# Freeing weight slots later, one more high buffer, and one unsplit fp32 chunk in each small expert of an MoE block

## The reference

```python
h = rms_norm(x, ffn_norm_g)                      # 512 x 1024
logits = h @ w_router + b_router                 # 32 experts, top 4 of each token, softmax over the 4
for e in range(32):                              # rows of h that chose expert e
    gu = xb @ w_gate_up[e] + b_gate_up[e]        # 1024 -> 2048
    gate, up = split(gu); gate = min(gate, 7); up = clip(up, -7, 7)
    act = (up + 1) * gate * sigmoid(1.702 * gate)
    y = (act @ w_down[e] + b_down[e]) * weight   # 1024 -> 1024, added to the token's row
```

## Time and profile before

| | |
|---|---|
| median of 3 runs | 1774.97 us (1774.8 to 1775.13) |
| profiled execution | 1766.66 us, span 1764.9 us |
| PE, DVE, ACT, POOL busy | 1698.8, 1381.7, 1200.8, 713.1 us |
| granted TensorE clock | 1.00 of full speed in the expert stage |
| moved by DMA | 504.64 MB, of them 384 chunks of 1 MB of expert weights |

### The profile page before, as it was taken

The page is one execution under the profiler, slowest core; times in us unless marked ns, Lnnn a source line. Parts: engine busy times, 40 slices in busy tenths (PEclk is TensorE's granted clock), DMA queues, the critical chain, the costliest instruction groups (busy, mean ns, idle before and its releaser), DMA issues.

```text
span 1764.9 us, 24895 instructions
## 1 busy us (share of the span) xinstructions
PE 1698.8 (96%) x8477; PEld 1346.8 (76%) x8477; DVE 1381.7 (78%) x1048; ACT 1200.8 (68%) x967; POOL 713.1 (40%) x344
## 2 busy tenths in 40 slices
PE   6999999999999999999999999999999999999998
PEld 5878889777888987767767767767767767767776
DVE  4666776755334389999999999999999999999984
ACT  5565555433223368788788788788788788788775
POOL 6124233550000072355465365365365365365110
PEclk9999999999999999999999999999999999999999
DMA  5443343433336469999999999999999999999951
GB/s 177 122 129 85 121 122 107 121 108 119 96 96 231 164 218 397 391 404 392 399 402 392 399 401 392 402 406 388 404 404 391 405 400 398 402 400 395 408 201 49
DMA packets 150865, 504.64 MB, mean 286 GB/s; under 512 B 12733, under 2 KB 73285, under 8 KB 117173
## 3 DMA queue, kind: packets, MB, share of 16 engines
q1 hardware_dynamic: 141652, 478.49, 70.0%
q0 software_dynamic: 9104, 25.28, 6.0%
q10 hardware_dynamic: 48, 0.07, 0.0%
HBM read 487.63 MB, written 20.28 MB: 288 GB/s over the span
## 4 chain that ended last, share of the span: by engine, by line
PE 68%; DVE 14%; issue 9%; ACT 6%; POOL 2%; DVEq 0%; ACTq 0%; POOLq 0%
PE gu_ps L2395 13%; DVE split_l L1928 9%; PE gu_ps L2147 8%; PE gu_ps L2149 8%; PE gu_ps L2148 8%; PE dn_ps L2453 7%; PE gu_ps L2399 7%; PE dn_ps L2459 3%; ACT split_h L1303 3%; PE gu_ps L2409 2%; PE dn_ps L2652 1%; PE gu_ps L2652 1%; PE et_ps L2381 1%; DVE up_sb L1915 1%; PE gu_ps L2169 1%
## 5 line engine op out<-in xcount | busy, mean ns | idle before, releaser
L1928 DVE TENSOR_TENSOR split_l<-ring,split_h 128x2048 fp32r<-128x2048 f32 x384 | 864.8, 2285 | 71.0 <-ACT split_h L1303 69.3
L1303 ACT ACTIVATE split_h<-ring 128x2048 fp32r<-128x2048 f32 x384 | 729.9, 1913 | 113.8 <-PE gu_ps L2399 62.7
L914 POOL COPY icur<-slots 96x1 int32 x30 | 282.8, 9428 | 412.3 <-PE et_ps L2381 410.1
L1536 DVE TENSOR_TENSOR w_lo<-w_raw,w_hi 128x2048 fp32r<-128x2048 f32 (+1 forms) x45 | 104.3, 2318 | 128.8 <-ACT w_hi L1035 122.6
L2409 PE MATMUL gu_ps<-split_l,xgT_h 128*128 128x512 f32 x480 | 139.6, 412 | 17.8 <-DVE split_l L1928 14.0
L2147 PE MATMUL gu_ps<-hT_h,w_hi 128*128 128x512 f32 x392 | 154.6, 394 | 0.6 <-DVE acc L1589 0.6
L2149 PE MATMUL gu_ps<-hT_h,w_lo 128*128 128x512 f32 x392 | 152.7, 390 | 0.0
L2148 PE MATMUL gu_ps<-hT_l,w_hi 128*128 128x512 f32 x392 | 152.6, 389 | 0.0
L2395 PE MATMUL gu_ps<-split_h,xgT_h 128*128 128x512 f32 x512 | 140.6, 396 | 0.9 <-DVE xgT_l L1934 0.9
L2399 PE MATMUL gu_ps<-split_l,xgT_h 128*128 128x512 f32 x512 | 137.2, 390 | 0.0
L2395 PE MATMUL gu_ps<-split_h,xgT_l 128*128 128x512 f32 x512 | 137.2, 390 | 0.0
(11 more groups left out here) (426 smaller groups left out, 3242.1 us busy)
## 6 DMA issues: line engine op xcount, KB each, us to landing
ring<-in_w_gate_up SPq DMA_DIRECT2D x256, 1024.0 KB, 8.0
ring<-in_w_down SPq DMA_DIRECT2D x128, 1024.0 KB, 9.2
w_raw<-in_w_in SPq DMA_DIRECT2D x28, 1024.0 KB, 5.9
arow<-acum_rows POOLq DMA_DIRECT2D x16, 512.0 KB, 6.5
w_raw<-in_w_ssd_out SPq DMA_DIRECT2D x8, 1024.0 KB, 5.4
w_raw<-in_w_in SPq DMA_DIRECT2D x9, 512.0 KB, 6.1
w_raw<-in_w_mix_out SPq DMA_DIRECT2D x4, 1024.0 KB, 7.9
wpg<-in_w_ple_gate SPq DMA_DIRECT2D x2, 2048.0 KB, 19.9
```

Source lines behind the costliest of these rows:

```text
L914: g.tensor_copy(icur[:, :], col).then_inc(idx_done, 1)
L1303: a.activation(split_h[s % SPLIT][:, :], ring[s % RING][:, :], ACT.Copy).then_inc(hi_done, 1)
L1536: v.tensor_tensor(w_lo[RAW_SLOT[n]][:, 0:size], w_raw[RAW_SLOT[n]][:, 0:size], w_hi[HI_SLOT[n]][:, 0:size].bitcast(F32), ALU.subtract).the ...
L1928: v.tensor_tensor(split_l[s % SPLIT][:, :], ring[s % RING][:, :], split_h[s % SPLIT][:, :].bitcast(F32), ALU.subtract).then_inc(lo_done, 1)
```

## The change

- `RING` becomes 8 and `SPLIT` 4. The low part is written over the ring slot that it was computed from (`ring_low` has the addresses of `ring`), and `split_l` goes away; its 24 KB and the space between make room for two more slots and the fourth `split_h`. Six of the slots (`FIRST`) lie where the ring lay, two behind the high buffers.
- A slot is given back to SP by `chunk_used` (PE is through) and no longer by `lo_done` (DVE is through). The first loads of the two new slots need no wait.
- In a small expert's gate-up, chunk k = 4 (`WHOLE`) is not split: PE multiplies the loaded float32 chunk by `xgT_h` (high and low part of the rows side by side) as four fp32 products (`whole_gate_up`). ACT and DVE leave that chunk out; `hi_done` and `lo_done` are raised by 2 at the chunk before it.
- Since 12 chunks are no longer a multiple of the ring, loops run over pairs of experts and step arguments become `(pair, offset)`; `slot_of` gives the slot.
- Orders: ACT does high part 10 before `gate` or the fold copy, high part 12 before `turned_high`, and 13 and 14 before the copies out of `dn_ps`; DVE does low part 10 before `up` and low part 12 before `turned_low`.

```diff
-RING = 6
-SPLIT = 3
+RING = 8
+FIRST = 6
+WHOLE = 4
+SPLIT = 4
...
-        ring = [here(f"ring{i}", [P, 2 * DM], F32) for i in range(RING)]
+        ring_off = top[0]
+        ring = [here(f"ring{i}", [P, 2 * DM], F32) for i in range(FIRST)]
+        top[0] = ring_off
+        ring_low = [here(f"ring_low{i}", [P, 2 * DM], F32R) for i in range(FIRST)]
...
         split_h = [here(f"split_h{i}", [P, 2 * DM], F32R) for i in range(SPLIT)]
-        split_l = [here(f"split_l{i}", [P, 2 * DM], F32R) for i in range(SPLIT)]
...
+        def slot_of(e, i):
+
+            return (in_pair(e)[1] * CHUNKS + UP + i) % RING
...
             def gate_up(j, e, i, of, k, first=False):
 
-                slot = (UP + i) % RING
+                slot = slot_of(e, i)
                 if not first:
-                    sp.wait_ge(lo_done, chunk_at(j, e, i) + 1)
+                    sp.wait_ge(chunk_used, chunk_at(j, e, i) + CHUNKS - RING + 1)
...
-            for k in range(RING):
+            for k in range(FIRST):
                 gate_up(0, 0, k - UP, 0, k, True)
...
-            for k in range(RING, UP):
-                gate_up(0, 0, k - UP, 0, k)
+            for k in range(FIRST, UP):
+                gate_up(0, 0, k - UP, 0, k, True)
...
-            def high(j, e, i):
+            def high(j, e, i, parts=1):
 
                 at, s = chunk_at(j, e, i), UP + i
-                act.wait_ge(e_loaded[s % RING], raw_loaded(j, e, i))
+                act.wait_ge(e_loaded[slot_of(e, i)], raw_loaded(j, e, i))
                 act.wait_ge(chunk_used, at + CHUNKS - SPLIT + 1)
-                a.activation(split_h[s % SPLIT][:, :], ring[s % RING][:, :], ACT.Copy).then_inc(hi_done, 1)
+                a.activation(split_h[s % SPLIT][:, :], ring[slot_of(e, i)][:, :], ACT.Copy).then_inc(hi_done, parts)
...
                 def rest(e, more, rows_in, rows_act, folds=None):
 
-                    turned_high(t0 + 3 + e * 2, xgT_h, rows_in, 1.0 if more else 1.0 / ALPHA)
-                    for i in range(12, 14):
-                        high(j, e, i)
+                    n = number(e)
+                    high(j, e, 12)
+                    turned_high(t0 + 3 + n * 2, xgT_h, rows_in, 1.0 if more else 1.0 / ALPHA)
+                    high(j, e, 13)
+                    high(j, e, 14)
                     if folds is not None:
-                        half_down_out(e, e)
-                    high(j, e, 14)
+                        half_down_out(e, n)
+                    whole = isinstance(j, int) and rows_in == HALF
+                    high(j, e, CHUNKS + WHOLE - 1, 2 if whole else 1)
...
                     if more:
+                        if not whole:
+                            high(j, e, CHUNKS + WHOLE)
...
                 def expert(e, more, rows_in=ROWS, folds=None):
 
-                    gate(j, e, UP - 1, n0 + e + 1)
                     high(j, e, 10)
+                    gate(j, e, UP - 1, n0 + number(e) + 1)
                     high(j, e, 11)
...
                 def half_expert(e, folds):
 
-                    halves_out(e, e + 1)
                     high(j, e, 10)
+                    halves_out(e, number(e) + 1)
+                    high(j, e, 11)
                     half_gate(folds)
-                    high(j, e, 11)
...
-                v.tensor_tensor(split_l[s % SPLIT][:, :], ring[s % RING][:, :], split_h[s % SPLIT][:, :].bitcast(F32),
-                                ALU.subtract).then_inc(lo_done, 1)
+                v.tensor_tensor(ring_low[slot_of(e, i)][:, :], ring[slot_of(e, i)][:, :],
+                                split_h[s % SPLIT][:, :].bitcast(F32), ALU.subtract).then_inc(lo_done, parts)
...
+                    low(j, e, 12)
+                    if rows_in == HALF:
+                        turned_low(t0 + 3 + n * 2, xgT_h[:, :, HALF:P], xgT_h, HALF)
+                    else:
+                        turned_low(t0 + 3 + n * 2, xgT_l[:, :, 0:ROWS], xgT_h, ROWS, 1.0 if more else 1.0 / ALPHA)
+                    for i in range(13, 15):
                         low(j, e, i)
+                    low(j, e, CHUNKS + WHOLE - 1, 2 if rows_in == HALF else 1)
...
                 def expert(e, more, half_next=False):
 
-                    up(ROWS, chunk_used, chunk_at(j, e, UP - 1) + CHUNKS + 1, n0 + e + 1)
                     low(j, e, 10)
+                    up(ROWS, chunk_used, chunk_at(j, e, UP - 1) + CHUNKS + 1, n0 + number(e) + 1)
                     low(j, e, 11)
...
+            def whole_gate_up(e, i, k):
+
+                raw = ring[slot_of(e, i)]
+                pe.wait_ge(e_loaded[slot_of(e, i)], raw_loaded(0, e, i))
+                alone(pe)
+                for b in range(4):
+                    o = t.matmul(gu_ps[:, b * 512:b * 512 + 512], xgT_h[:, k, :].bitcast(F32),
+                                 raw[:, b * 512:b * 512 + 512], start=False, stop=False)
+                o.then_inc(chunk_used, 1)
...
                 for k in range(2, UP):
-                    half_gate_up(e, k, k)
-                down_free(e)
+                    if k == WHOLE:
+                        whole_gate_up(e, k, k)
+                    else:
+                        half_gate_up(e, k, k)
+                down_free(n)
```

More of the change, by code:

```diff
@@ L374, in program @@
         split_h = [here(f"split_h{i}", [P, 2 * DM], F32R) for i in range(SPLIT)]
-        split_l = [here(f"split_l{i}", [P, 2 * DM], F32R) for i in range(SPLIT)]
+        ring_off = top[0]
+        ring += [here(f"ring{i}", [P, 2 * DM], F32) for i in range(FIRST, RING)]
+        top[0] = ring_off
+        ring_low += [here(f"ring_low{i}", [P, 2 * DM], F32R) for i in range(FIRST, RING)]
         xgT_off = top[0]
@@ L520, in program @@
         pen_done, last_idx = sem("pen_done"), sem("last_idx")
-        e_loaded = [sem(f"e_loaded{i}") for i in range(RING)]
+        e_loaded = [sem(f"e_loaded{i}") for i in range(FIRST)] + yT_loaded[0:RING - FIRST]
         hi_done, lo_done, et_hi = sem("hi_done"), sem("lo_done"), sem("et_hi")
@@ L584, in conv_tile, with in_pair, number @@
             return {"X": 4 * g + (key[2] if len(key) > 2 else 0), "B": 16 + g, "C": 20 + g}[key[0]]
+        def in_pair(e):
+            return (0, e) if isinstance(e, int) else e
+        def number(e):
+            return e if isinstance(e, int) else e[0] * 2 + e[1]
         def chunk_at(j, e, i):
-            return j * NE * CHUNKS + e * CHUNKS + UP + i
+            pair, off = in_pair(e)
+            return j * NE * CHUNKS + pair * (2 * CHUNKS) + off * CHUNKS + UP + i
+        def slot_of(e, i):
+            return (in_pair(e)[1] * CHUNKS + UP + i) % RING
         def raw_loaded(j, e, i):
-            return (j * (NE * CHUNKS // RING) + e * (CHUNKS // RING) + (UP + i) // RING + 1) * 16
+            pair, off = in_pair(e)
+            before = 1 if slot_of(e, i) >= FIRST else 0
+            return (j * (NE * CHUNKS // RING) + pair * (2 * CHUNKS // RING) + (off * CHUNKS + UP + i) // RING + 1 + before) * 16
         def passes(eng):
@@ L729, in weights, with expert_loads @@
                     sp.wait_ge(order_done, 1)
-                with sp.Fori(1 if ahead else 0, NE - 1) as e:
-                    of, after = (position(sp, e), position(sp, e + 1)) if ahead else (e, e + 1)
-                    bias_parts(j * NE + e + 1, after)
+                def expert_loads(e):
+                    n = number(e)
+                    of, after = (position(sp, n), position(sp, n + 1)) if ahead else (n, n + 1)
+                    bias_parts(j * NE + n + 1, after)
                     for k in range(UP):
@@ L736, in weights @@
                         down(j, e, UP + r, of, r)
+                with sp.Fori(0, PAIRS) as i:
+                    for off in (1, 2) if ahead else (0, 1):
+                        expert_loads((i, off))
+                if not ahead:
+                    expert_loads(NE - 2)
                 of = position(sp, NE - 1) if ahead else NE - 1
@@ L1425, in one_pass @@
                     with act.Fori(0, PAIRS - 1) as i:
-                        expert(i * 2 + 2, True, HALF, i * 2 + 2)
-                        half_expert(i * 2 + 3, i * 2 + 3)
+                        expert((i, 2), True, HALF, i * 2 + 2)
+                        half_expert((i, 3), i * 2 + 3)
                     expert(NE - 2, False, folds=NE - 2)
                 else:
-                    with act.Fori(0, NE - 2) as e:
-                        expert(e, True)
+                    with act.Fori(0, PAIRS) as i:
+                        expert((i, 0), True)
+                        expert((i, 1), True)
                     expert(NE - 2, False)
@@ L2430, in half_down @@
                             o = t.matmul(dn_ps[:, b * 512:b * 512 + 512], actT_h[:, 2 * r + k, :],
-                                         part[s][:, k * DM + b * 512:k * DM + b * 512 + 512],
-                                         start=r == 0 and k == 0 and part is split_h, stop=False)
```

(4 more changed lines are left out.)

87 lines of the change are left out of this document (43 added, 44 removed).

## The result

The changed kernel took 1791.53 us (median of 5; 1786.98 to 1794.78) beside 1774.97 for the kernel before: ratio 1.009, 95% interval 1.0075 to 1.011. It is 16.6 us slower. The forecast was 18 us faster; of its cases the third rival (late folds, slower) lies nearest.

What follows compares the result with a forecast made beforehand. PE was taken to bound the full half of each expert pair, DVE the small half. Transfers of 64.2 plus 0.4 us gave 64.6 against 65.8 us, 1.2 us a pair, 18 us over 15 pairs: 1757 us, range 1725 to 1780.

Steps and rivals of the forecast that it cites:

- the third rival: Expert pair: fold copy and turned parts queue behind late loads, PE waits; 67.1 us a pair, 1795 us; 20%.
- What bounds the kernel before: Expert stage: PE sets the full half of a pair, DVE the small half; 65.78 us a pair.
- Fp32 products: Unsplit chunk of small gate-up: four products cost 3.43 us, adding 1.6 us to PE, 61.8 us a pair.
- Low parts in place: DVE's subtraction written over the loaded chunk costs nothing; bounds 0 and 0.2 us a pair.
- Four high buffers: Small half: one more chunk of lead, 2.7 us, removes PE's whole wait for DVE; bounds 0 and 5.6 us a pair.
- Transfers: Expert pair: transfers become the next bound, slower beside gathers and scatters; 64.2 us a pair.
- I take 64.2: Transfer time per pair: 16.5 us at 355 GB/s, the rest at 426 GB/s.
- The bound named as the upper one: Transfers per pair if the DMA engines have nothing left at any time: 65.8 us.
- Worth nothing itself: Ring loads start 0.7 to 1.7 us earlier, no gain, since ACT waited for loads only 5.2 us in 780.
- Orders: ACT and DVE reordering in each pair costs 0.2 us; bounds 0 and 2.0 us.
- The other half of the rival: Late-fold case: PE's wait for DVE only halves, to 2.8 us a pair.
- Its milder case: Late-fold case with half of PE's waits at the join and next gate-up: 1782 us.

Runs made afterwards that it cites:

- f_before_light: Kernel before, loading only half of each expert down chunk, engine work kept: 1766.66 us, ratio 0.9999.
- q: Changed kernel with half of each down chunk loaded, old ACT and DVE orders and three high buffers: 1759.16 us, ratio 0.9958.
- h: Changed kernel with half of each down chunk loaded and the old ACT and DVE orders: 1745.08 us, ratio 0.988.
- g: Changed kernel with half of each down chunk loaded, engine work kept: 1738.18 us, ratio 0.9837.
- o: Changed kernel with half of each down chunk loaded and three high buffers instead of four: 1859.31 us, ratio 1.0474.
- l_gap: Changed kernel, fold copy before high part 10, turned parts before parts 12, DVE waiting until POOL has issued each gather: 1788.08 us, ratio 1.0073.
- r_gap_no_scatter: l_gap with the scatters of results left out: 1743.89 us, ratio 0.9868.
- i_no_whole_gap: Changed kernel without the unsplit chunk, DVE waiting once a pair until POOL has issued the gather: 1782.51 us, ratio 1.0088.
- c_no_whole: Changed kernel without the unsplit chunk, all 12 chunks of a small expert split: 1852.70 us, ratio 1.0479.
- j_less_pe: Changed kernel with fold copy before high part 10 and four of twelve products per full-expert chunk left out: 1781.98 us, ratio 1.0074.

## Why the prediction was wrong

- **What bounds the kernel before: right.** f_before_light shows it.
- **Fp32 products: right.** 3.60 us of records. The second group of four products behind them starts 4.35 us after their own start, 0.91 of it the first group's, so they cost 3.4. PE's own 61.8 us measured about 62.5.
- **Low parts in place: right.** 369 subtractions with a mean of 2285 ns, as before.
- **Four high buffers: the mechanism right, the size near.** The whole wait for DVE went, as taken. With light loads and in this order of adding, ring, low parts in place and unsplit chunk give 7 us, the buffer 14, the orders 7 (q, h, g). They don't add up in any order: the new orders without the buffer cost 1859 us (o).
- **Transfers: this step failed, and it is the main one.** "I take 64.2" was too low. The sum had five stretches of 3.3 us, 16.5 us, at 355 GB/s and all else at 426. By the prediction's own figures all else ran at 412 (20.3 MB in 49.3 us), so 426 rested on the guess that the rest was a lack of loads. l_gap, with its loads always queued, shows 28 us at 351 and the rest at 424: 66.5 us a pair. The slices of 380 to 400 around the dips had been counted as undisturbed. The bound named as the upper one, 65.8, was the one to take; the changed kernel took 66.4. The engines' share of 1.01 over the pair pointed that way, but it could not prove it, since f_before_light shows that the transfers did not set that pair's length. The reading that fits all runs is that in the kernel before hand-over and transfers had nearly the same length, so relieving the first could give nothing. The 358 GB/s that the Trainium skill, DMA: Bandwidth & Descriptors, "Where 436 GB/s comes from", gives for the HBM side is no bound here either: 394 to 402 were sustained over 780 us (l_gap, r_gap_no_scatter). The same section derives the figure as one core's half of what two share, and this program runs on one core.
- **"Worth nothing itself" (slots freed by PE): wrong in its use.** ACT's small waits for loads were taken from a kernel in which ACT was held back by its buffers. With one more it reaches the next load before that has landed: 5.2 us became 36.5, 72 and 125.
- **Orders: 0.2 us a pair was too little.** This is the third rival's place, the fold copy behind high part 10, and it decides as that rival said, on late landings. The price was 28.9 us of PE's waits over the run (1.9 a pair), and the clock behind them; putting the copy first gives 8 us back (1.0097 to 1.005). The turned low part cost 0.66 us once a pair, not 1.5. The other half of the rival, PE's wait for DVE halving only (2.8 us), did not come; without it the rival's pair is 64.3 us and not 67.1. That its 1795 lies near the 1791.53 measured is therefore partly luck. Its milder case, 1782, doesn't follow from its terms either: half of 2.5 us in place of 2.5 gives 65.85 us a pair, 1776.
- **POOL: not in the prediction at all.** It did not decide this result, but it decides between its variants (1.048 against 1.009).

## What to carry to other kernels

When two resources take nearly the same time for a period, relieving one shows nothing: cut the other's load alone (half the bytes, same engine work) to see how far each goes, before building. The floor of transfers is read from a kernel in which loads are always queued (here to about 1%: 66.5 against 65.8 us), not from the best stretch of one in which they are not. What is moved behind an instruction that waits for a load inherits the wait of that load, however short it was in the kernel before.

## What the hardware showed unexpectedly

- **DVE shuts POOL out.** A copy of 96 int32, 0.18 us when free, took 10 to 28 us (some 10 in the kernel before already, with no effect there), and the issue of a gather 14 to 29 us instead of 1.0, while DVE subtracted without a gap, both inputs in SBUF. The gap made for POOL removed it (i_no_whole_gap). The Trainium skill, SBUF — State Buffer, "Who interferes with whom", says that a DVE instruction with two SBUF inputs contends with a GpSimd instruction that reads SBUF; the traces agree on the copies. For the issue of a DMA by POOL the same section infers that such a DVE instruction doesn't hold it up, and the 14.05 us of the gather in c_no_whole, which reads its row numbers from SBUF, disagree. Nor did POOL get in between the six subtractions of a run, 13.29 us long. A short instruction with one input in PSUM did not always let it in either: a turned low part of 0.68 us lies within the copy of 12.54 us in c_no_whole.
- **An idle PE can be dear twice.** 3.77 us at the join were followed by 4.7 us at a granted clock of 0.50. In j_less_pe, with a sixth of PE's work taken away, the clock was 0.90 over 780 us and no time came back.
- **Leaving out the indirect scatters gave more than their bytes:** 2.5 us a pair or more for 0.5 MB, which at 398 GB/s are 1.3 (r_gap_no_scatter). POOL's work on them went too.
